# Identity products on TensorE in two waits ahead of the first projection pair

## The reference

```
mod = silu(c) @ ada_w + ada_b
sh1, sc1, gt1, sh2, sc2, gt2 = split(mod, 6)
h = rms_norm(x, pre_g1) * (1.0 + sc1) + sh1
proj = h @ w_in            # 1024 x 4608: q, k, v, gMLP u, v, two gates
...                        # attention, gMLP, merge, output projection
...                        # PEER: product-key top-k, experts, second residual
```

## Time and profile before

| What | Before |
|---|---|
| Median of three runs | 1550.05 us |
| Lowest and highest of the three | 1549.62 and 1551.42 us |
| Span of the profiled execution | 1549.6 us, no time of its own beside it is listed |
| PE busy | 1466.4 us, 95% of the span |
| Mean granted TensorE clock | 0.983 of full speed |
| DVE busy | 1326.8 us, 86% |
| ACT and POOL busy | 673.2 us (43%) and 787.1 us (51%) |

### The profile page before, as it was taken

One profiled execution on the slowest core, in us unless ns is written; L12 is line 12 of the kernel. 1 busy time (PEld: TensorE's weight loads), 2 busy tenths in 40 slices (PEclk: granted clock), 3 DMA queues, 4 the chain that ended last, 5 costly groups with the idle time before them and its releaser, 6 DMA issues.

```text
span 1549.6 us, 25331 instructions
## 1 busy us (share of the span) xinstructions
PE 1466.4 (95%) x7847; PEld 1261.3 (81%) x7847; DVE 1326.8 (86%) x2654; ACT 673.2 (43%) x1255; POOL 787.1 (51%) x733
## 2 busy tenths in 40 slices
PE   4999999999989778889999999999999999999996
PEld 3777767868577577779999999999999999999995
DVE  5878645346999989799999999999999999999998
ACT  5232456322157567534444434444444444444443
POOL 1010000000059857677767667767667667667662
PEclk8999999999999989999999999999999999999998
DMA  9895211440021256899999999999999999999994
GB/s 344 317 388 193 81 55 55 149 181 1 1 110 55 75 227 258 339 402 402 401 397 401 398 369 403 390 375 402 391 365 402 396 377 402 381 379 402 383 384 157
DMA packets 164991, 448.84 MB, mean 290 GB/s; under 512 B 14683, under 2 KB 50675, under 8 KB 164284
## 3 DMA queue, kind: packets, MB, share of 16 engines
q1 hardware_dynamic: 108732, 243.33, 42.4%
q0 software_dynamic: 56192, 204.66, 33.7%
HBM read 423.72 MB, written 22.32 MB: 288 GB/s over the span
## 4 chain that ended last, share of the span: by engine, by line
PE 78%; DVE 13%; DMA 3%; issue 2%; ACT 2%; POOL 1%; SPq 0%; ACTq 0%; DVEq 0%; POOLq 0%
PE bank L942 15%; PE bank L1205 9%; PE bank L1204 9%; PE bank L1203 9%; PE bank L1227 7%; PE bank L1225 7%; PE bank L1226 7%; PE bank L1217 4%; PE bank L1218 4%; PE bank L1125 2%; PE bank L1038 2%; DMA w_scratch<-staged 1%; PE bank L885 1%; DVE top_i L1937 1%; DVE scores L1938 1%
## 5 line engine op out<-in xcount | busy, mean ns | idle before, releaser
L778 POOL DMA_INDIRECT v_rows<-v_exp,small x192 | 258.0, 1344 | 91.2 <-POOL small L774 51.0
L778 POOL DMA_INDIRECT u_rows<-u_exp,small x192 | 255.9, 1333 | 92.8 <-POOL small L774 52.0
L1203 PE MATMUL bank<-h_hi,u_hi 128*128 128x320 f32 x944 | 291.1, 308 | 0.7 <-ACT staged L1500 0.7
L1204 PE MATMUL bank<-h_lo,u_hi 128*128 128x320 f32 x944 | 291.7, 309 | 0.0
L1205 PE MATMUL bank<-h_hi,u_lo 128*128 128x320 f32 x944 | 291.7, 309 | 0.0
L1227 PE MATMUL bank<-v_hi,g_both 128*128 128x512 f32 x512 | 204.2, 399 | 0.0
L1603 ACT ACTIVATE v_hi<-v_raw 128x1024 fp32r<-128x1024 f32 x128 | 135.5, 1058 | 157.6 <-PE bank L1227 116.4
L1225 PE MATMUL bank<-v_hi,g_both 128*128 128x512 f32 x512 | 203.2, 397 | 0.0
L1226 PE MATMUL bank<-v_lo,g_both 128*128 128x512 f32 x512 | 203.2, 397 | 0.0
L1204 PEld LDWEIGHTS bank<-h_lo,u_hi 128*128 128x128 f32 x944 | 177.1, 188 | 6.2
L1203 PEld LDWEIGHTS bank<-h_hi,u_hi 128*128 128x128 f32 x944 | 177.2, 188 | 5.7 <-ACT staged L1500 0.9
(11 more groups left out here) (255 smaller groups left out, 2923.6 us busy)
## 6 DMA issues: line engine op xcount, KB each, us to landing
v_raw<-v_exp SPq DMA_DIRECT2D x128, 512.0 KB
u_raw<-u_by_key SPq DMA_DIRECT2D x120, 512.0 KB
ada_blk<-ada_w SPq DMA_DIRECT2D x22, 1024.0 KB, 10.9
ring<-w_in SPq DMA_DIRECT2D x18, 1024.0 KB, 10.1
w_row<-w_scratch SPq DMA_DIRECT2D x128, 128.0 KB
w_scratch<-staged SPq DMA_DIRECT2D x2, 4096.0 KB, 17.0
xr<-x SPq DMA_DIRECT2D x8, 512.0 KB, 6.3
ring<-w_branch SPq DMA_DIRECT2D x4, 1024.0 KB, 5.1
```

The lines of the kernel that those rows point to most:

```text
L778: pool.indirect_dma_start(out=rows[s], out_offset=None, in_=table, in_offset=bass.IndirectOffsetOnAxis(ap=ix[:, s:s + 1], axis=0))\
L1203: pe.matmul(o, u_hi[:, r, k], h2_hi[:, k], start=(k == 0), stop=False)
L1204: pe.matmul(o, u_hi[:, r, k], h2_lo[:, k], start=False, stop=False)
```

## The change

A new function issues n products of the 128x128 identity with itself. They go into the bank that job 3 of the first block uses, and nothing reads them: pair 0 starts that bank afresh. The function is called with 40 between `columns(0)` and `columns(2)`, and with 34 between `columns(2)` and `pair(0)`.

```
+            def idle_products(n):
+
+                o = start("in", IN_ORDER[0], 3)
+                for _ in range(n):
+                    pe.matmul(o[:, 0:P], ident[:, :], ident[:, :], start=True, stop=True)
+
             columns(0)
+            idle_products(40)
             columns(2)
+            idle_products(34)
             pair(0)
             pair(1)
             pair(2, range(3))
```

## The result

The changed kernel takes 1555.87 us (median of 7 runs, 1552.95 to 1556.78) against 1550.05 us (7 runs, 1549.09 to 1551.66). The medians lie 5.8 us apart. The forecast was 1553.6 us, 3.5 us more, in a range of 1550.4 to 1556.0; it had 0.63 on slower by over 0.2%.

What follows compares the result with a forecast made beforehand. PE was taken as the unbroken chain from pair 0 to `columns(3)`. Products overrunning both gaps start pair 0 6.1 us later, the full clock returns 2.9 us: 3.2, taken as 3.5, giving 1553.6 us (range 1550.4 to 1556.0).

Steps and rivals of the forecast that it cites:

- The price of a product: In both gaps before pair 0, each identity product is two records and takes 0.223 us at the full clock.
- The rival of one record each: Products in both gaps cost 0.113 us like transposes and fit; 4.0 us less, 1546.1 us; chance 0.05.
- The clock: The products hold PE's clock at 1.00 through both gaps and the pairs, from 18 to 56 us.
- rival fallen: Clock not held: it falls at 24.7 during the products, pair 0 is 20.2 us late, 1570.2 us; chance 0.06.
- No overlap: Product records in the gaps take their full 0.272 us each, pair 0 27 us late, about 1577 us; chance 0.03.
- The times of the steps: On PE, `columns(2)` starts at 30.0, pair 0 at 38.4, pair 1 at 43.9 and `columns(3)` at 58.6 us.
- What becomes of the 3.2 us: Behind pair 1, later stages neither hide nor add to the 3.2 us delay; the whole chain shifts.
- The size: Whole kernel 3.5 us slower, taken between 3.2 and 4.5 us: 1553.6 us.
- the forecast's own case: Whole kernel slower, ending between 1551.5 and 1555.5 us; chance 0.78.
- the gain from the full clock: Pair 0's first 14 matmuls take 3.21 us in place of 6.11: 2.90 us less.
- the sum: Up to pair 1: pair 0 starts 6.1 us later, its first matmuls are 2.9 us shorter, 3.2 us late.
- the start of the products: In the first gap, the first product starts at about 21.1 us, as `columns(0)` ends at 21.20.

Runs made afterwards that it cites:

- transp: The changed kernel with its 40 and 34 products each made a transpose of the identity; ratio 0.9986 against the kernel before, 2.2 us less.
- double: The changed kernel with 80 and 68 products in place of 40 and 34; ratio 1.0137 against the kernel before, +21.2 us.
- base1 to base4: The kernel before without any edit, four more profiled executions; `columns(3)` starts at 54.73, 54.92, 54.55 and 56.16 us.
- again: The changed kernel itself, 40 and 34 products, measured on another chip; ratio 1.0029 against the kernel before, +4.5 us.
- fit: The changed kernel with 21 and 19 products in place of 40 and 34; 1547.88 us against 1551.36 for the kernel before, ratio 0.9980.
- even: The changed kernel with 32 and 28 products in place of 40 and 34; ratio 1.0021 against the kernel before, +3.3 us.
- first: The changed kernel with the 40 products of the first gap only, none in the second; ratio 1.0018 against the kernel before, +2.8 us.

## Why the prediction was right

**The price of a product** was right: two records, 9.04 / 40 = 0.226 us and 7.70 / 34 = 0.226 us against 0.223. The rival of one record each fell in the trace, and transp shows what it would have given.

**The clock** was right: it held at 1.00 through both gaps and the pairs (rival fallen).

**No overlap** of the products' records fell with the same rows; the 0.324 us that the prediction estimated from the Trainium skill ("TensorE: Matmul & The Clock Gate", Back-to-back issue gap, and "FP8 and Floating Point Precision", TensorE Precision Notes) is not seen (0.226).

**The times of the steps** were right within 0.15 us in the profiled execution: `columns(2)` at 30.15 (forecast 30.0), pair 0 at 38.39 on the timeline (38.4), pair 1 at 43.93 (43.9), `columns(3)` at 58.64 (58.6).

**What becomes of the 3.2 us** was right: they are in the chain at 74.84 unchanged, and double shows that 16.6 us more pass through as well. Rest, in the table, stays between 1493.1 and 1495.4 us in all ten executions there, with no order by count. In base1 to base4, the kernel before, it is 1494.4, 1493.3, 1494.3 and 1495.3 us: the same spread with no product at all.

**The size** was too small: 3.5 forecast, 5.0 measured (3.3 to 6.7), 4.5 on the second chip (2.6 to 6.5). The median of 1555.87 us is only 0.1 us inside the range and above the 1555.5 to which the forecast's own case was said to reach; that the range held was in part luck. The term that was mis-sized is the gain from the full clock, taken as 2.90 us and lowered by only 0.3. The prediction named the direction, that the first profile's low clock was long and that another execution might lose only 1.6 us, and then stayed close to the one profile. Four more executions give 2.0 to 2.9, 2.4 in the mean. With 2.4, the sum is 6.1 - 2.4 = +3.7. A smaller term is the start of the products, taken as 21.1 from the same profile. With the mean end of `columns(0)`, 21.57, in place of the changed profile's 21.11, pair 0 starts at 38.39 + 0.46 = 38.85, against a mean of 32.50 in before: 6.35 - 2.4 = +3.9. The profiles agree: `columns(3)` starts at 59.02 in the mean of changed and again, 3.9 us behind 55.16. In fit the gain is 0.9 from the earlier start and 2.4 from the clock, 3.3 against 3.1 measured.

**The starting point** was misread, without harm to the sum. The prediction set the span of 1549.6 beside the median of 1550.05, as 0.4 us under it. A time is some 2.1 us more than its span, so that the profiled execution was a slow one of before.

**What stays open.** Some 1 us of the changed kernel's 5.0 lies beyond the sum and within its interval. For even the same sum gives 3.0 - 2.4 = +0.6 (+0.9 by the start of `columns(3)` against the mean of before), less than the lower end of what was measured (1.9) and less than the 2.4 us by the spans. Its one profile is nearer to the sum (1550.7 against a mean span of 1549.4 for the five executions of before). In the profiles the remaining differences lie behind `columns(3)` (the changed kernel's rest is 1.0 us above that of before, that of again 0.3 below). That they come from falls of the clock at one place or another in the middle, and that these are more frequent or dearer for some counts, is only a guess; no run here tests it.

## What to carry to other kernels

Work that only keeps TensorE's clock up must end before the real work is ready: here 21 and 19 products gained 3 us and 40 and 34 lost 5, and each product beyond the gap cost its full 0.226 us. Count its records in the trace, not its instructions, since a float32 product is two and a transpose one. Expect a gain where PE is the last to come behind the gap, as at pair 0, and take its size from several executions.

## What was not expected of the hardware

The clock's return after an idle stretch is not the same in executions of one kernel: the pairs ran at the low clock for 10 to 14 matmuls, 4.3 to 6.1 us, in five executions. Transposes of the identity keep the clock at 1.00 as products do (transp: 1.00 in both gaps). And a gap of 4.5 us between bursts was enough for it to fall, even right behind 10 us of dense products at the full clock (first): there the granted clock is 1.00 until 32, 0.92 from 32 to 33 and 0.50 from 33, with PE idle since 31.1, while in the earlier trace rows it fell 3.5 us after PE went idle.
